# Head and key norms kept as columns of tokens, and the linear recurrence and its neighbours moved to earlier units of mixer 2's projection

## The chip, the cores and the metric

One core of a Trainium2 chip runs the whole program. The metric is the device time of one execution in microseconds (us). TensorE does matmuls, VectorE and ScalarE work elementwise, GpSimd and SyncE here only issue DMAs.

## The reference

512 tokens with 1024 features pass two blocks. The first has two layers: a layer norm with modulation from a vector c, a projection to 22 tiles of 128 features, attention (8 query heads and 2 key heads of 64, each normed over its 64 features and rotated), a short convolution, a Fourier mix, and an output projection with another layer norm. The second has two layers, each feed-forward, mixer, feed-forward. The mixer of its last layer (mixer 2) is the one that the change touches:

```python
q = _axial_rope(_rms_norm(q.reshape(b, s, N_Q_HEADS, HEAD_DIM), q_gain[l]), row_ang, col_ang)
k = _axial_rope(_rms_norm(k.reshape(b, s, N_KV_HEADS, HEAD_DIM), k_gain[l]), row_ang, col_ang)
...
kk = _l2norm(_heads(k * rwkv_k_k, RWKV_HEADS))
y = _rwkv7_scan(rh, decay, kh, vh, kk, a)
xb = _causal_dwconv(lx, lru_conv_w) + lru_conv_b
log_a = -LRU_C * gate_r * jax.nn.softplus(-lru_lambda)
mult = jnp.sqrt(jnp.maximum(-jnp.expm1(2.0 * log_a), 0.0))
hl = _linear_scan(jnp.exp(log_a), mult * gate_i * xb)
y_lru = hl * jax.nn.gelu(ly)
return jnp.concatenate([y_rwkv, y_lru], -1) @ w_out
```

## The kernel before

Features lie on partitions, tokens along the free axis, 512 wide. A weight unit is 128 output features by 1024 inputs. SyncE loads units into a ring of four; ScalarE writes a rounded copy (`high`, L1609), VectorE the remainder (`low`, L2215), and TensorE forms each of the 8 input tiles' product as three matmuls of 512 columns, 24 for a unit (`part` in the projections does some of the 8 tiles, so that other matmuls can stand between its two halves). Every engine's order is written out by hand, and engines meet through counting semaphores (`pe_done`, `act_done`, `dve_done`, `tile_copied`, `unit_used`, `unit_split`).

**Head norms** (`first_block`, both layers). Units 8 to 12 are the key tile and four query tiles of two heads each, number i = 0 to 4. ScalarE evicts unit 8+i and squares it. In the middle of unit 9+i TensorE multiplies the squares by a constant that has 1/64 within a head (`rms`), which leaves the mean on every partition of the head. ScalarE takes the root of 128x512 (`rsd`), VectorE its reciprocal and one multiplication (`normed`, L2414 and L2198), in its turn 8+i, and TensorE at the end of unit 11+i the matmul `rot` of the rotation, which VectorE finishes in `roped`. In layer 0 the turns 0 to 7 of VectorE also hold three products each for the modulation (`ada`, L2391), whose operands come by DMA from GpSimd's queue.

**Mixer 2** (`odd_projection`, 22 units, then `rwkv`). Units 0 to 3 are the input of the linear recurrence (LRU), unit 4 two low ranks, 5 to 8 keys, 9 to 12 values, 13 a gate, 14 to 17 queries, 18 to 21 the gelu input. VectorE evicts each unit (L3004). Around that stand:

- `lru_gates(i)` on TensorE at the end of unit 5+i, two sigmoids of them on ScalarE (banks 6 and 7, so the next gates wait for them); then exponentials (`la`) in unit 10, squares and tanh in 11, relu and roots (`lmult`) in 12, and on VectorE `lru_root` in 11 and `lru_scan` in 13 and 14.
- `low_rank` in units 7 to 9 and their sigmoids; `key_square` in 7 to 9; `key_squares` in the middle of unit 10 sums the squares of a head, four matmuls with 32 output rows; a root of 128x512 (`kksd`) and its reciprocal (`krstd`, L3018); `key_roots` spreads the result at the ends of units 11 and 12, two banks in turn, so the second pair waits for `unit_keys` of the first.
- `cumulate`, `keys_decayed`, `queries_decayed`, `lru_hidden`, `gelu_inner` and `bonus` on VectorE in units 10 to 21 and after them.

`rwkv` first builds the chunk matrices of four token tiles tt (`matrices`), transposes (`tokens`, waits for each `bonus`), and VectorE masks them; `matrices(tt)` waits for the masks of tt-1.

The reader needs these lines most:

```python
def rms(i):
    pe.wait_ge(*act_done("rsq", l, i))
    step(mm(PS[6][:], cst("blk64"), tile(17 + i)), "rms", l, i)
...
def key_squares():
    pe.wait_ge(*act_done("rgate", 2))
    for j in range(4):
        pe.wait_ge(*act_done("kksq", j))
        ins = mm(PS[6][32 * j:32 * j + 32, :], cst("blk1")[:, 32:96:2], tile(22 + j))
```

Of the kernel before, what the change touches and what calls it, by code (L numbers as in the profile page):

```python
# [132 lines left out]
def write_program(nc, known, x_in, w_k, w_d0, w_d1, w_shift, w_ada, c_in, vec_in, cst_in, small_in, dft_in, out):  # L133

    with ExitStack() as ctx:
# [27 lines left out]
        NORM = sb("norm_columns", [P, 12])  # L163
        PS = [ctx.enter_context(nc.psum_tensor(f"bank{i}", [P, T], F32)) for i in range(8)]
# [275 lines left out]
        def _(pe):  # L440
# [79 lines left out]

            def rms_of(norm, *parts):
# [81 lines left out]
            def first_block(l):  # L603
# [33 lines left out]
                for j in range(K0 + 1, FILLING):  # L637
# [6 lines left out]
                    if j - K0 >= 3:  # L644
                        rot(j - K0 - 3)

# [6 lines left out]
                def scores(p):  # L653
                    t, qt = p // 4, p % 4
                    pe.wait_ge(*dve_done("rope", l, t + 1))
                    if p == 0:
                        pe.wait_ge(*act_done("turn", name, 0))
                    if p >= 2:
# [532 lines left out]
            def odd_projection():  # L1191
# [40 lines left out]
                def key_squares():  # L1232
                    pe.wait_ge(*act_done("rgate", 2))
                    for j in range(4):
                        pe.wait_ge(*act_done("kksq", j))
                        ins = mm(PS[6][32 * j:32 * j + 32, :], cst("blk1")[:, 32:96:2], tile(22 + j))
                    step(ins, "kk2")

                def key_roots(j):
# [3 lines left out]
                    step(mm(PS[6 + j % 2][:], cst("pick")[:, col(j)], tile(22)), "kroot", j)  # L1243
# [6 lines left out]
                for j in range(LEAD, N_ODD):  # L1250
                    part(j, 0, 4)
                    if j == LEAD + 1:
                        spread(("pre", name))
                    if j == 7:
                        low_rank(0)
                    elif j == 10:
                        key_squares()
                    part(j, 4, KT)
                    if 5 <= j <= 8:
                        lru_gates(j - 5)  # L1260
# [7 lines left out]
                    elif j in (11, 12):  # L1268
                        key_roots(2 * j - 22)
                        key_roots(2 * j - 21)  # L1270
                    elif j in (20, 21):
                        bonus(2 * j - 40)
                        bonus(2 * j - 39)
# [265 lines left out]
        def _(act):  # L1539
# [126 lines left out]
            def first_block(l):  # L1666
# [14 lines left out]
                for j in range(K0, FILLING):  # L1681
                    evict(j, ACT.Copy)
                    if j < V0:
                        i = j - K0
                        act.wait_ge(*pe_done("rms", l, i))
                        a(tile(17 + i), PS[6][:], ACT.Sqrt, "rsd", l, i, bias=v("eps6"), chain=False)
# [268 lines left out]

            def odd_projection():
# [30 lines left out]
                def gelu_gate(i):  # L1987
                    act.wait_ge(*dve_done("gelu0", i))
                    a(gelu_input(i), gelu_input(i), ACT.Sigmoid, "gelu", i, scale=float(np.sqrt(8 / np.pi)), chain=False)

                for j in range(N_ODD):
                    if j > LEAD:
# [26 lines left out]
                    if 5 <= j <= 8:  # L2019
                        i = j - 5  # L2020
                        act.wait_ge(*pe_done("lgate", i))
# [1446 lines left out]
```

## Time and profile before

| | before |
|---|---|
| median of 3 runs | 2745.77 us (2742.93 to 2746.58) |
| profiled execution, its own time | 2746.36 us |
| its span, first to last instruction | 2744.40 us |
| TensorE busy | 2670.0 us, 97% |
| VectorE busy | 1545.2 us, 56% |
| ScalarE busy | 1028.5 us, 37% |
| mean granted clock of TensorE | 0.991 of full speed |

The profile is one execution; its own time is 0.59 us over the median. In the timeline a row is one or several instructions of one kind; the name left of the arrow is written, those right of it are read; "128\*64 128x512" is 128 contraction rows, 64 output rows, 512 columns. A plain fp32 matmul shows as two records.

### The profile page before, as it was taken

The numbers are of one execution on the slowest core, as the hardware profiler recorded it, in microseconds if no ns is written. First come the engines' busy times: TensorE is split into PE (matmuls) and PEld (weight loads), VectorE is DVE, ScalarE is ACT, GpSimd is POOL, SyncE is SP. The second block draws the span as 40 slices with busy tenths as digits, with TensorE's granted clock in tenths as the row PEclk, the third lists the DMA queues.
The fourth block names the chain that finished last, engine by engine and source line by source line (L and its number), as shares of the span: only waits on it lengthen the run. The fifth ranks groups of instructions, "written<-read, shape, count | busy, mean of one in ns | idle before, by whom it ended". The sixth has DMA issues, their size and how long they took to land.

```text
span 2744.4 us, 38094 instructions
## 1 busy us (share of the span) xinstructions
PE 2670.0 (97%) x15846; PEld 2135.2 (78%) x15846; DVE 1545.2 (56%) x2232; ACT 1028.5 (37%) x1534; POOL 19.0 (1%) x39
## 2 busy tenths in 40 slices
PE   8999999999999999999999999999999898999998
PEld 5766776678888788877888887888876797788886
DVE  6976867575244664645543447424475975653344
ACT  3354536442223354224322334222346422532322
POOL 0100000000000000000000000000000000000000
PEclk9999999999999999999999999999999999999999
DMA  8611321122332321101323232233222100232322
GB/s 339 224 54 67 115 95 61 55 85 87 104 102 75 102 84 40 41 31 62 109 84 114 82 106 90 87 106 100 77 99 70 48 19 2 92 104 87 109 77 69
DMA packets 71451, 243.93 MB, mean 89 GB/s; under 512 B 7921, under 2 KB 8177, under 8 KB 70257
## 3 DMA queue, kind: packets, MB, share of 16 engines
q1 hardware_dynamic: 66240, 222.11, 24.7%
q0 software_dynamic: 5040, 19.40, 1.9%
q8 instruction: 126, 2.06, 0.3%
q14 instruction: 45, 0.36, 0.0%
HBM read 239.38 MB, written 2.10 MB: 88 GB/s over the span
## 4 chain that ended last, share of the span: by engine, by line
PE 88%; DVE 7%; DMA 2%; ACT 2%; issue 1%; SPq 0%; DVEq 0%; ACTq 0%
PE bank L442 86%; DMA work<-w_ada 2%; DVE work L2198 1%; PE bank L674 1%; DVE residual L2198 1%; DVE weights_low L2215 1%; DVE work L2391 1%; ACT work L1543 1%; ACT weights_high L1609 0%; DVE work L2414 0%; ACT normed L1543 0%; DVE work L2530 0%; DMA residual<-x_in 0%; DVE work L2283 0%; DVE constants L3004 0%
## 5 line engine op out<-in xcount | busy, mean ns | idle before, releaser
L442 PE MATMUL bank<-normed,weights_high 128*128 128x512 f32 x4848 | 1530.6, 397 | 11.0 <-ACT normed L1543 11.0
L442 PEld LDWEIGHTS bank<-normed,weights_high 128*128 128x128 f32 x4848 | 904.2, 189 | 234.9 <-issue 51.9
L442 PE MATMUL bank<-normed,weights_low 128*128 128x512 f32 x2424 | 949.3, 392 | 0.0
L1609 ACT ACTIVATE weights_high<-ring 128x1024 fp32r<-128x1024 f32 (+2 forms) x431 | 420.7, 979 | 833.0 <-PE bank L442 830.7
L2215 DVE TENSOR_TENSOR weights_low<-ring,weights_high 128x1024 fp32r<-128x1024 f32 (+2 forms) x431 | 484.0, 1125 | 408.7 <-ACT weights_high L1609 405.2
L442 PEld LDWEIGHTS bank<-normed,weights_low 128*128 128x128 f32 x2424 | 457.6, 189 | 96.2
L442 PE MATMUL bank<-hidden,weights_high 128*128 128x512 f32 x1408 | 433.7, 389 | 0.0
L442 PEld LDWEIGHTS bank<-hidden,weights_high 128*128 128x128 f32 x1408 | 264.5, 188 | 54.7
L2590 DVE TENSOR_TENSOR silu_gate<-bank,rstd 128x512 f32<-128x512 f32 x176 | 120.9, 691 | 325.0 <-PE bank L442 324.9
L442 PE MATMUL bank<-hidden,weights_low 128*128 128x512 f32 x704 | 274.2, 390 | 0.0
L442 PEld LDWEIGHTS bank<-hidden,weights_low 128*128 128x128 f32 x704 | 132.2, 188 | 27.4
L442 PE MATMUL bank<-work 64*64 64x64 f32 (+6 forms) x1600 | 146.2, 316 | 5.5 <-DVE work L3076 4.1
L1543 ACT ACTIVATE work<-bank 128x512 f32<-128x512 f32 (+2 forms) x175 | 97.5, 582 | 112.1 <-PE bank L442 84.7
L442 PEld LDWEIGHTS bank<-work 64*64 64x64 f32 (+2 forms) x1600 | 83.3, 148 | 46.0 <-issue 26.8
L1543 ACT ACTIVATE hidden<-silu_gate 128x512 fp32r<-128x512 f32 x88 | 55.6, 632 | 152.3 <-DVE silu_gate L2596 152.3
L2578 DVE TENSOR_TENSOR hidden<-silu_gate,hidden 128x512 fp32r<-128x512 f32 x88 | 61.0, 693 | 61.5 <-ACT hidden L1543 61.5
L442 PE MATMUL bank<-work,constants 128*128 128x512 f32 (+5 forms) x328 | 73.0, 376 | 17.5 <-DVE work L2198 4.9
L1543 ACT ACTIVATE silu_gate<-bank 128x512 f32<-128x512 f32 (+1 forms) x40 | 23.9, 598 | 111.4 <-PE bank L442 111.4
L1543 ACT ACTIVATE silu_gate<-silu_gate 128x512 f32<-128x512 f32 x88 | 54.5, 619 | 27.9 <-DVE silu_gate L2590 27.9
L442 PEld LDWEIGHTS bank<-work,constants 64*64 64x64 f32 (+2 forms) x328 | 34.3, 156 | 36.2 <-issue 9.3
L1543 ACT ACTIVATE work<-work 128x512 f32<-128x512 f32 (+1 forms) x78 | 47.5, 628 | 39.6 <-DVE work L2525 12.6
L2596 DVE TENSOR_TENSOR silu_gate<-silu_gate 128x512 f32<-128x512 f32 x88 | 60.3, 686 | 0.8
(270 smaller groups left out, 1919.1 us busy)
## 6 DMA issues: line engine op xcount, KB each, us to landing
ring<-w_k SPq DMA_DIRECT2D x303, 512.0 KB, 3.7
ring<-w_d SPq DMA_DIRECT2D x64, 384.0 KB, 3.0
ring<-w_d SPq DMA_DIRECT2D x64, 320.0 KB, 2.9
work<-w_ada POOLq DMA_DIRECT2D x32, 512.0 KB, 6.4
work<-w_shift SPq DMA_DIRECT2D x4, 1024.0 KB, 10.9
work<-w_ada SPq DMA_DIRECT2D x7, 512.0 KB, 17.2
constants<-cst_in SPq DMA_DIRECT2D x1, 2176.0 KB, 21.0
residual<-x_in SPq DMA_DIRECT2D x4, 512.0 KB, 6.5
```

Of the source, the lines that this page charges most:

```text
L442: return pe.matmul(o, lhsT, rhs, start=start, stop=stop, skip_group_check=True)
L674: ins = pe.transpose(PS[4 + s][:, col(st)], probs(p, s)[:, col(st)], cst("ident"))
L1543: ins = nc.scalar.activation(o, i, func, bias=bias, scale=scale, **extra)
L1609: nc.scalar.activation(WH[:, u % SPLIT, 0:w], RING[:, u % SLOTS, 0:w], ACT.Copy).then_inc(unit_high, 1)
L2198: return ve.scalar_tensor_tensor(out=o, in0=a, scalar=s, in1=b, op0=op0, op1=op1)
L2215: ve.tensor_tensor(WL[:, u % SPLIT, 0:w], RING[:, u % SLOTS, 0:w], WH[:, u % SPLIT, 0:w].bitcast(F32), ALU.subtract).then_inc(unit_split, 1)
L2391: d(ve.scalar_tensor_tensor(out=w, in0=w, scalar=v("one"), in1=BIG[:, 22:24, :], op0=ALU.mult, op1=ALU.mult, accum_out=MOD[:, l, 8 * part ...
L2578: d(ve.tensor_tensor(HID[:, 12 + p, :], GATE[:, 2 + p % 2, :], HID[:, p, :].bitcast(F32), ALU.subtract), "hidden", f, q, p, chain=False)
L2590: d(ve.tensor_tensor(GATE[:, 2 * w + p % 2, :], ffn_bank("pair", q, p, w)[:], RSTD[:, 1, :], ALU.mult), "scaled", f, q, p, w, chain=False)
L2596: d(ve.tensor_tensor(GATE[:, 2 + p % 2, :], GATE[:, 2 + p % 2, :], GATE[:, p % 2, :], ALU.mult), "gated", f, q, p, chain=False)
```

## The change

1. **Head norms.** `rms(i)` exchanges its operands: per token tile the squares are the stationary side, so the result has tokens on partitions and the heads in columns (4 matmuls of 128 columns in place of one of 512). Root and reciprocal are of 128x8 in place of 128x512. A new step `rms_spread(i)` at the end of unit 9+i brings the result back to features on partitions: 8 matmuls, each with 64 output rows and 128 columns, into bank 0. It waits for VectorE's reciprocal (`rrms`) and the last `normed`. `normed(i)` comes a turn later and reads bank 0.
2. **Key norms.** `key_squares` becomes 16 matmuls with 128 output rows and 32 columns; root and reciprocal are of 128x32; `key_roots` is 8 matmuls as above in place of one of 512 columns, at the ends of units 11 and 13.
3. **Linear recurrence.** The gates stand at the end of unit 5, the middle and end of 6 and the middle of 7; the exponentials in ScalarE's turn 7, squares and tanh in 8, relu and roots in 9, VectorE's roots in 9, the scans in 10 and 11.
4. **The rest of VectorE's steps** is about a unit sooner; `bonus` on TensorE comes after unit 19 and in the middle of 21. `gelu_inner` and `gelu_gate` of 2 and 3 stand behind the masks of the first token tile.

```diff
+            def spread_heads(bank, columns):
+
+                for tt in range(TT):
+                    for s in range(2):
+                        x = 2 * tt + s
+                        ins = mm(bank[64 * s:64 * s + 64, col(tt)], columns[:, x:x + 1].broadcast_to([P, 64]), cst("ident"))
+                return ins
...
                 def rms(i):
                     pe.wait_ge(*act_done("rsq", l, i))
-                    step(mm(PS[6][:], cst("blk64"), tile(17 + i)), "rms", l, i)
+                    for tt in range(TT):
+                        ins = mm(PS[6][:, col(tt)], tile(17 + i)[:, col(tt)], cst("blk64"))
+                    step(ins, "rms", l, i)
+
+                def rms_spread(i):
+                    pe.wait_ge(*dve_done("rrms", l, i))
+                    if i:
+                        pe.wait_ge(*dve_done("rn", l, i - 1))
+                    step(spread_heads(PS[0], HEAD_NORM[i % 2]), "rspread", l, i)
...
                     if j - K0 >= 3:
                         rot(j - K0 - 3)
+                    if j - K0 - 1 < 5:
+                        rms_spread(j - K0 - 1)
...
-                        ins = mm(PS[6][32 * j:32 * j + 32, :], cst("blk1")[:, 32:96:2], tile(22 + j))
+                        for tt in range(TT):
+                            x = 4 * j + tt
+                            ins = mm(PS[6][:, 32 * x:32 * x + 32], tile(22 + j)[:, col(tt)], cst("blk1")[:, 48:80])
...
-                    step(mm(PS[6 + j % 2][:], cst("pick")[:, col(j)], tile(22)), "kroot", j)
+                    step(spread_heads(PS[6 + j % 2], KEY_NORM[:, 8 * j:8 * j + 8]), "kroot", j)
...
+                    if j in (6, 7):
+                        lru_gates(2 * j - 11)
                     if j == 7:
                         low_rank(0)
                     elif j == 10:
                         key_squares()
+                    elif j == 21:
+                        bonus(2)
+                        bonus(3)
                     part(j, 4, KT)
-                    if 5 <= j <= 8:
-                        lru_gates(j - 5)
+                    if j in (5, 6):
+                        lru_gates(2 * j - 10)
...
                 for j in range(N_ODD):
+                    if j in (6, 7):
+                        lru_sigmoids(2 * j - 11)
                     if j > LEAD:
                         high(u0 + j + SPLIT)
...
-                    if j == 9:
-                        low_rank_gates(3)
-                        key_square(3)
-                        act.wait_ge(*pe_done("kk2"))
-                        a(tile(22), PS[6][:], ACT.Sqrt, "kksd", bias=v("eps6"), chain=False)
-                    elif j == 10:
+                    if j == 7:
                         act.wait_ge(*dve_done("lam"))
                         for i in range(4):
                             act.wait_ge(*act_done("lr", i))
                             a(GATE[:, i, :], tile(i), ACT.Exp, "la", i, scale=LRUV[:, 8 + i:9 + i], chain=False)
-                    elif j == 11:
+                    elif j == 8:
                         for i in range(4):
                             lru_decay_square(i)
                             a(tile(i), tile(i), ACT.Tanh, "ltanh", i, scale=LRUV[:, 12 + i:13 + i], chain=False)
-                        key_decays(0)
-                    elif j == 12:
+                    elif j == 9:
+                        low_rank_gates(3)
+                        key_square(3)
...
+                        act.wait_ge(*pe_done("kk2"))
+                        a(KEY_NORM[:], PS[6][:, 0:T:16], ACT.Sqrt, "kksd", bias=v("eps6"), chain=False)
...
+                    if K0 < j <= V0:
+                        dve.wait_ge(tile_copied, c0 + j)
+                        normed(j - K0 - 1)
                     if K0 <= j < V0:
-                        dve.wait_ge(tile_copied, c0 + j + 1)
-                        normed(j - K0)
+                        reciprocal_rms(j - K0)
```

How the orders move, at two places. First VectorE in layer 0, from the last operation on the modulation (128x8) through turns 8 and 9; `weights_low` is `low`. Before:

```order
L2198 SCALAR_TENSOR_TENSOR modulation<-modulation,vectors 128x8 [waits dve_steps]
L2215 TENSOR_TENSOR weights_low<-ring,weights_high 128x1024 [waits unit_used,unit_high]
L2414 RECIPROCAL work<-work 128x512 [waits act_steps,tile_copied]
L2198 SCALAR_TENSOR_TENSOR work<-work,vectors 128x512 [waits dve_steps]
L2215 TENSOR_TENSOR weights_low<-ring,weights_high 128x1024 [waits unit_used,unit_high,dve_steps]
L2414 RECIPROCAL work<-work 128x512 [waits act_steps,tile_copied,consts_in]
L2198 SCALAR_TENSOR_TENSOR work<-work,vectors 128x512 [waits dve_steps]
```

Now:

```order
L2231 SCALAR_TENSOR_TENSOR modulation<-modulation,vectors 128x8 [waits dve_steps]
L2248 TENSOR_TENSOR weights_low<-ring,weights_high 128x1024 [waits unit_used,unit_high]
L2453 RECIPROCAL head_norm<-head_norm 128x8 [waits act_steps]
L2248 TENSOR_TENSOR weights_low<-ring,weights_high 128x1024 [waits unit_used,unit_high]
L2231 SCALAR_TENSOR_TENSOR work<-work,vectors,bank 128x512 [waits pe_steps,tile_copied,consts_in]
L2453 RECIPROCAL head_norm<-head_norm 128x8 [waits act_steps]
L2248 TENSOR_TENSOR weights_low<-ring,weights_high 128x1024 [waits unit_used,unit_high]
```

The reciprocal keeps its place behind the turn's `low`; the multiplication moved behind the next `low` and now reads TensorE's bank.

Second ScalarE in mixer 2, turns 7 and 8 (`weights_high` is `high`, work<-constants the kept part of a unit, work<-bank the sigmoids of gates or low ranks, work<-work,vectors the squares of keys, silu_gate the exponentials). Before, turn 8:

```order
L1609 ACTIVATE weights_high<-ring 128x1024 [waits unit_used,w_loaded1]
L1543 ACTIVATE work<-constants,modulation 128x512 [waits tile_copied]
L1543 ACTIVATE work<-bank,vectors 128x512 [waits pe_steps]
L1543 ACTIVATE work<-bank,vectors 128x512
L1543 ACTIVATE work<-work,vectors 128x512 [waits dve_steps]
L1543 ACTIVATE work<-bank,vectors 128x512 [waits pe_steps]
L1543 ACTIVATE work<-bank,vectors 128x512
```

Now, from the exponentials at the end of turn 7 to the first squares and tanh of turn 8:

```order
L1571 ACT_TABLE_LOAD [waits act_steps]
L1571 ACTIVATE silu_gate<-work,lru_vectors 128x512 [waits dve_steps]
L1571 ACTIVATE silu_gate<-work,lru_vectors 128x512 [waits act_steps] x3
L1637 ACTIVATE weights_high<-ring 128x1024 [waits unit_used,w_loaded1]
L1571 ACTIVATE work<-constants,modulation 128x512 [waits tile_copied]
L1571 ACTIVATE work<-work,vectors 128x512 [waits dve_steps]
L1571 ACT_TABLE_LOAD
L1571 ACTIVATE work<-bank,vectors 128x512 [waits pe_steps]
L1571 ACTIVATE work<-bank,vectors 128x512
L1571 ACTIVATE work<-silu_gate 128x512 [waits act_steps]
L1571 ACTIVATE work<-work,lru_vectors 128x512
```

The four exponentials, the squares and tanh (three more pairs follow) and two table loads now stand ahead of turn 9.

## Rows read from the trace of the kernel before

**Rows 1.** Timeline, TensorE, layers 0 and 1 (start us, us, engine, line, what, [idle before and releaser]).
```profile
94.04 1.02 PE L442 MATMUL bank<-work,constants 128*128 128x512 f32 x2
...
111.25 1.13 PE L442 MATMUL bank<-work,constants 128*128 128x512 f32 x2 [0.72 <-DVE work L2198]
...
122.68 1.31 PE L442 MATMUL bank<-work,constants 128*128 128x512 f32 x2 [3.95 <-DVE work L2421]
...
380.02 1.02 PE L442 MATMUL bank<-work,constants 128*128 128x512 f32 x2
383.65 1.02 PE L442 MATMUL bank<-work,constants 128*128 128x512 f32 x2
```

**Rows 2.** Timeline, VectorE, layer 0, turns 7 and 8.
```profile
105.83 0.17 DVE L2198 SCALAR_TENSOR_TENSOR modulation<-modulation,vectors 128x8 f32<-128x8 f32 x1
105.92 1.22 DVE L2215 TENSOR_TENSOR weights_low<-ring,weights_high 128x1024 fp32r<-128x1024 f32 x1
107.06 3.35 DVE L2414 RECIPROCAL work<-work 128x512 f32<-128x512 f32 x1
```

**Rows 3.** Timeline, TensorE: existing matmuls of the shapes that come in.
```profile
172.04 3.65 PE L442 MATMUL bank<-work 128*64 128x512 f32 x16
...
1028.49 1.05 PE L442 MATMUL bank<-constants,work 128*128 128x1 f32 x8
1029.40 0.70 PE L442 MATMUL bank<-normed,weights_high 128*128 128x512 f32 x2
...
1088.87 4.54 PE L442 MATMUL bank<-work 128*64 128x128 f32 x64
```

**Rows 4.** Timeline, TensorE, projection of mixer 2, without its units.
```profile
2054.13 1.88 PE L442 MATMUL bank<-work,small_weights 128*128 128x512 f32 x4
...
2085.58 1.99 PE L442 MATMUL bank<-work,small_weights 64*128 64x512 f32 x8
2090.44 1.60 PE L442 MATMUL bank<-work,constants 128*32 128x512 f32 x8
...
2101.39 1.99 PE L442 MATMUL bank<-work,constants 128*128 128x512 f32 x4 [0.95 <-DVE work L3018]
2113.00 3.37 PE L442 MATMUL bank<-work,constants 128*128 128x512 f32 x4 [4.14 <-DVE work L2198]
```

**Rows 5.** Timeline, ScalarE, projection of mixer 2.
```profile
2059.59 1.25 ACT L1543 ACTIVATE work<-bank,vectors 128x512 f32<-128x512 f32 x2
...
2085.75 1.06 ACT L1609 ACTIVATE weights_high<-ring 128x1024 fp32r<-128x1024 f32 x1 [3.75 <-PE bank L442]
...
2087.94 2.40 ACT L1543 ACTIVATE work<-bank,vectors 128x512 f32<-128x512 f32 x4
...
2090.96 1.28 ACT L1543 ACT_TABLE_LOAD   x1
...
2098.08 2.56 ACT L1543 ACTIVATE silu_gate<-work,lru_vectors 128x512 f32<-128x512 f32 x4
...
2103.66 0.61 ACT L1543 ACTIVATE work<-silu_gate 128x512 f32<-128x512 f32 x1
...
2104.79 0.61 ACT L1543 ACTIVATE work<-silu_gate 128x512 f32<-128x512 f32 x1
```

**Rows 6.** Timeline, VectorE, eviction of units 10 and 13.
```profile
2095.03 0.69 DVE L3004 TENSOR_TENSOR constants<-bank,rstd 128x512 f32<-128x512 f32 x1 [5.71 <-PE bank L442]
...
2122.15 0.69 DVE L3004 TENSOR_TENSOR constants<-bank,rstd 128x512 f32<-128x512 f32 x1 [8.64 <-PE bank L442]
```

**Rows 7.** Timeline, TensorE, end of the projection and the first chunks.
```profile
2167.77 1.88 PE L442 MATMUL bank<-silu_gate,constants 128*128 128x512 f32 x4
...
2180.09 3.69 PE L442 MATMUL bank<-work 64*64 64x128 f32 x64 [2.79 <-DVE work L3076]
...
2187.89 1.98 PE L442 MATMUL bank<-work 64*64 64x128 f32 x64 [0.64 <-DVE work L3076]
```

**Rows 8.** Stretches: length; PE, PEld, DVE, ACT, POOL busy; granted clock; DMA share, GB/s.
```profile
2179.00:2181.00 2.00, 0.91 (x18) 0.91 (x21) 2.00 (x6) 0.00 (x0) 0.00 (x0) 0.50 0.00 0
```

More of the change, by code:

```diff
@@ L1267, in odd_projection @@
                         low_rank(3)
[L1268 to L1273, printed above, removed]
+                    elif j in (11, 13):
+                        key_roots(j - 11)
+                        key_roots(j - 10)
+                    elif j == 19:
+                        bonus(0)
+                        bonus(1)
                 pe.wait_ge(tile_copied, c0 + N_ODD)
@@ L1954, in lru_lambda, with gelu_gate @@
                 a(LRUV[:, 0:4], LRUV[:, 0:4], ACT.Exp, "lam", scale=-1.0, chain=False)
+            def gelu_gate(i):
+                act.wait_ge(*dve_done("gelu0", i))
+                a(gelu_input(i), gelu_input(i), ACT.Sigmoid, "gelu", i, scale=float(np.sqrt(8 / np.pi)), chain=False)
             def odd_projection():
@@ L2410, in normed, with reciprocal_rms @@
                 def normed(i):
+                    dve.wait_ge(*pe_done("rspread", l, i))
+                    x = tile(ROPED[i])
+                    d(stt(x, x, v("qg" if i else "kg", l), PS[0][:], ALU.mult, ALU.mult), "rn", l, i, chain=False)
+                def reciprocal_rms(i):
                     dve.wait_ge(*act_done("rsd", l, i))
[L2413 to L2415 removed]
+                    r = HEAD_NORM[i % 2]
+                    d(ve.reciprocal(r[:], r[:]), "rrms", l, i, chain=False)
                 def roped(i):
@@ L3017, in odd_projection @@
                         dve.wait_ge(*act_done("kksd"))
-                        d(ve.reciprocal(tile(22), tile(22)), "krstd", chain=False)
+                        d(ve.reciprocal(KEY_NORM[:], KEY_NORM[:]), "krstd", chain=False)
+                        lru_scan(0)
+                        lru_scan(1)
                         cumulate(0)
                     elif j == 11:
+                        lru_scan(2)
+                        lru_scan(3)
                         cumulate(1)
-                        for i in range(4):
-                            lru_root(i)
                     elif j == 12:
@@ L3045, in odd_projection, with gelu_inner @@
                         queries_decayed(3)
-                    elif j >= 20:
-                        lru_hidden(j - 20)
-                        gelu_inner(j - 20)
-                        bonus(j - 20)
-                for i in (2, 3):
-                    lru_hidden(i)
-                    gelu_inner(i)
-                    bonus(i)
+                    elif j == 20:
+                        for i in (0, 1):
+                            lru_hidden(i)
+                            gelu_inner(i)
+                            bonus(i)
+                    elif j == 21:
+                        for i in (2, 3):
+                            lru_hidden(i)
+                            bonus(i)
+                    if j == 9:
+                        for i in range(4):
+                            lru_root(i)
+            def gelu_inner(j):
+                x = gelu_input(j)
+                dve.wait_ge(*act_done("gelu0", j))
+                dve.wait_ge(*dve_done("lhidden", j))
+                d(stt(x, gelu_square(j), 1.0, x, ALU.add, ALU.mult), "gelu0", j, chain=False)
             def lru_out(j):
@@ L3066, in rwkv @@
                     else:
-                        for j in ((1, 2) if tt == 1 else (3,) if tt == 2 else ()):
-                            lru_out(j)
+                        if tt == 1:
+                            gelu_inner(2)
+                            gelu_inner(3)
+                        lru_out(tt)
                         low(UNIT0["mixout1"] + tt - 1)
```

72 lines of the change are left out of this document (31 added, 41 removed).

## The prediction

> **What bounds the kernel now.** I read the busy times first: TensorE is busy 97% of the span, so whatever it gains or loses goes into the time almost whole, and work on VectorE or ScalarE counts only where TensorE waits for it. Then I read the waits of TensorE at the places of the change. In layer 0 it waits 0.72 us and 3.95 us for VectorE, which does the reciprocals of 3.35 us in a row [rows 1, 2]. In mixer 2 it waits 0.95 us for the reciprocal of the key norms and 4.14 us for the first two unit keys [rows 4]. At the end of the projection VectorE's chain holds it up: from 2167.77, when unit 21 has ended, to 2187.89, when the third chunk's matrices start, 20.1 us pass [rows 7]. A wait costs more than itself. After the one of 2.79 us the granted clock is 0.50, the lower level of 1.2 GHz, and 64 records take 3.69 us that take 1.98 later [rows 7, 8]: 1.7 us more for a long wait.
>
> **A pace for all that follows.** In layer 1 half a unit and a matmul of 512 columns take 3.63 us, 380.02 to 383.65 [rows 1]. Of that the matmul, two records of fp32, is 0.87, since four records with nothing between take 1.88 and their last end reaches some 0.15 further [rows 4]. Half a unit is 2.75 and a unit 5.5.
>
> **Head norms, price on TensorE.** Turning `rms` round leaves 512 columns in all: nothing. `rms_spread` adds 8 matmuls, 16 records of 64 output rows, ten times in all. Two neighbours of that shape run beside each other: 16 records of 512 columns take 3.65 [rows 3], 8 times 0.43 in place of 16. The nearest row in width, 64 records of 128 columns in 4.54, gives 1.1 for 16 [rows 3]; going into the other shape and back I put at 0.2, an estimate by the 0.2 that the 3.65 has over 8 times 0.43. I take 1.3 each. The bounds are 0.9 (a quarter of 3.65) and 2.0 (no overlap, 16 times 0.11 from the records of one column, plus 0.2).
>
> **Layer 0.** This step decides. `rms_spread(0)` waits for the reciprocal of VectorE's turn 8, and TensorE asks for it at the end of unit 9. `rms(0)` starts at 94.04 in the middle of that unit [rows 1], so the unit ends at 94.04 + 3.63 = 97.7. VectorE is then far behind: its turns 0 to 7 hold the modulation, whose last operation starts at 105.83, and after the turn's `low` (1.22) the reciprocal starts at 107.06 [rows 2]. Nothing in that chain is shortened by the change. A reciprocal of 8 columns ends about 0.2 later (an operation of 8 columns takes 0.17 [rows 2]), so TensorE waits from 97.7 to 107.3, 9.6 us, all units behind it too. Before, the first result of VectorE that it needed was `normed(0)` at the end of unit 11, two units later. The sum for layer 0: 9.6 for the wait, 1.7 for the clock, 5 × 1.3 = 6.5 for the spreads, less 0.72 + 3.95 + 1.7 for the waits that go. They go since the reciprocals of 3.35 are gone and every later `rot` finds `normed` done: **+11.4 us**. With the wait over, ScalarE's root, VectorE's `low` and the small reciprocal fit into the half unit between `rms` and `rms_spread` (0.6 even for 512 columns [rows 5], 1.22 and 0.2, against 2.75), so the four later spreads don't wait.
>
> **Layer 1.** VectorE is in step there. Five spreads, no wait: **+6.5 us**.
>
> **Mixer 2, to the end of unit 21.** Gates 1 move to the middle of unit 6 and need the banks that ScalarE empties by its two sigmoids of gates 0. Gates 0 start at 2054.13; the middle of unit 6 is 2 × 0.87 + 2.75 later, 2058.6. The sigmoids run from 2059.59 to 2060.84, where they stand in ScalarE's turn 5 before as now [rows 4, 5]: +2.3. From there all of TensorE is 2.3 later; unit 9, which ended at 2085.58 after all four gates [rows 4], ends at 2087.9, unit 7 two units and a `low_rank` (half of 1.99) before, 2075.7 or so.
>
> `key_squares`, in the middle of unit 10, waits for ScalarE's last square of a key. Before it found it nearly done. Now ScalarE has more ahead of it. From 2075.7 it does three turns of high, kept and square (2085.75 to 2087.94 is 2.19 each, 6.6), a fourth square (0.6), eight sigmoids (four start to start in 2.3 us, 4.6), four exponentials (2.56), four pairs of square and tanh (2103.66 to 2104.79, 4 × 1.13 = 4.5) and two table loads (2 × 1.28 = 2.6) [rows 5]. That is 21.5 us: 2097.2, the sigmoids that it waits for first at 2095.4. TensorE is there at 2087.9 + 1.99 + 2.75 = 2092.7: a wait of 2.7 before the first matmuls. They are 32 records of 128 output rows; records of that shape with a single column start 0.11 apart (eight from 1028.49 to 1029.40 [rows 3]), so 32 take 3.5, in place of the 1.7 from 2090.44 to half a unit (2.75) before the eviction at 2095.03 [rows 4, 6]. Together 2.7 + 3.5 − 1.7 = +4.5, and 1.7 for the clock. The Trainium skill (TensorE: Matmul & The Clock Gate, Back-to-back issue gap) gives some 60 cycles to a matmul of up to 64 columns; by that the 32 would take 0.8 us and the total be 2.7 lower. The row with 0.11 decides for me, as every record here brings new weights of 128 columns.
>
> Four `key_roots` at 1.3 for 0.87: +1.7. What goes: 0.95 and 4.14, and the low clock after it (2113.00 to the eviction at 2122.15 is 9.15, for 2 × 0.87 + 5.5: 1.9) [rows 4, 6], and a small wait of `bonus`: −7.2. The second pair of roots behind unit 13 finds the keys within 1 us, since the scans now lie ahead of them on VectorE: 0, up to +1. Sum: 2.3 + 4.5 + 1.7 + 1.7 − 7.2 = **+3.0 us**.
>
> **The end of the projection.** Two of the `bonus` matmuls move before the end of unit 21, so I compare from unit 21 with all four done: before, 2167.77 + 1.74 = 2169.5 to 2187.89, 18.4 us [rows 7]. Now VectorE has, behind that point, one eviction, two pairs of `lru_hidden` and `bonus`, one `lru_out` and eight masks. With 0.69 for an operation of 512 columns [rows 6], 0.6 or so from start to start, and half for a mask of 256, that is 0.7 + 4 × 0.6 + 0.7 + 8 × 0.35 = 6.6; the matrices of tile 1 start then. VectorE goes on with two gelu steps, a `lru_out`, a `low` and eight masks, 1.3 + 0.6 + 1.2 + 2.8 = 5.9, waits some 0.3 for a transpose, and the matrices of tile 2 start. That is 12.9, all of it worked out from those rows, in place of 18.4: **−5.5 us**. The later cycles don't change; VectorE had slack there for one more `lru_out`.
>
> **Two waits between.** The wait of 2.3 at gates 1 and one of about 2.2 before the matrices of tile 1 are shorter than any after which I saw the low clock (2.79). I count half of 1.7 for each: **+1.7 us**.
>
> **Sum.** 11.4 + 6.5 + 3.0 − 5.5 + 1.7 = +17.1 us on the profiled execution's 2746.36: 2763.5. It lay 0.6 above the median of the runs, so I say **2763 us**.
>
> **The rivals.**
>
> *Spreads without overlap, slower still.* Fourteen spreads at 2.0 in place of 1.3: +9.8, **2773 us**. For it: each switch of shape may wait for the array to empty. The skill says so (TensorEngine Tiling (Array Packing), Key Properties: changing the tiling mode drains TensorE); the 3.65 in rows 3 holds such a switch and bounds it at some tenths. Against it: these rows. 0.14.
>
> *ScalarE keeps up in mixer 2.* If its chain to the last square is shorter than TensorE's (it decides at 2092.7), the waits of 2.7 and 2.3 and the low clocks there go, −2.7 − 1.7 − 2.3 − 0.85: **2755 us**. For it: ScalarE is busy only 37% of the span. Against it: the sum of 21.5 us has no idle in it. 0.12.
>
> *Not slower: no answer is asked for before it is there.* The mechanism is that VectorE's turn 8 in layer 0 comes in time; it decides whether its reciprocal is over by 97.7. Then 9.6 + 1.7 go, and in mixer 2 the waits of the rival above: 2763 − 11.3 − 7.5 = **2744 us**, 1.4 under the median; with the spreads at 0.9 it would be 2739. For it: the work removed from VectorE, ten reciprocals of 3.35, is far more than what is added. Against it: all of that work lies behind 105.83 in layer 0, and the modulation ahead of it waits for DMAs that nothing here speeds up. 0.09, split evenly over faster and the same.
>
> **How the numbers follow.** The forecast has 0.65. 2751 to 2773 holds it with the bounds of a spread (ten of them and four at 0.9 are −5.6) and most of the second and third case. 0.2% is 5.5 us, about what a measurement of this kernel can tell from no change; slower by more than that starts at 2751.3, and all cases but the last are there. Faster 0.05, the same 0.06, slower 0.89.
>
> **What would show it.** In the profile after: a wait of TensorE of about 9.6 us for a VectorE reciprocal at 97.7 in layer 0, and none in layer 1; ten groups of 16 records of 64 output rows, each about 1.3 us; in mixer 2 a wait near 2.3 us at the second gates, one of 2 to 3 us ahead of the 32 records of the key squares, no wait of 0.95 or 4.14; the matrices of tile 1 at 6.6 us after the end of unit 21. The forecast is wrong if layer 0 shows no long wait, if a spread takes 2 us, or if ScalarE's last square of keys comes before TensorE is in the middle of unit 10.

## The result, and the profile after

| | before | after |
|---|---|---|
| median of 5 runs | 2744.42 us (2742.0 to 2746.58) | 2757.46 us (2754.98 to 2761.96) |
| profiled execution, its own time | 2746.36 us | 2754.98 us |
| TensorE busy | 2670.0 us | 2679.2 us |
| VectorE busy | 1545.2 us | 1509.3 us |

The ratio of the runs is 1.0049, 95% interval 1.0038 to 1.0060: **slower by 13 us**, where 17 on a base of 2746.4 was forecast. The busy times of the page after:

```profile
PE 2679.2 (97%) x16146; PEld 2148.8 (78%) x16146; DVE 1509.3 (55%) x2232; ACT 1024.6 (37%) x1534; POOL 19.0 (1%) x39
```

VectorE has 36 us less to do, and the whole is slower even so; TensorE has 9 us more. Layers 0 and 1 on TensorE, first the ends of the two stretches in the kernel before (the first scores of layer 0, rms(0) and the first scores of layer 1):

```profile
145.72 1.13 PE L442 MATMUL bank<-work 64*128 64x512 f32 x4
...
363.70 1.02 PE L442 MATMUL bank<-work,constants 128*128 128x512 f32 x2
...
408.64 1.13 PE L442 MATMUL bank<-work 64*128 64x512 f32 x4
```

The same timeline of the kernel after:

```profile
93.39 1.05 PE L444 MATMUL bank<-constants,work 128*128 128x128 f32 x8
...
105.32 1.97 PE L444 MATMUL bank<-constants,head_norm 128*64 128x128 f32 x16 [8.14 <-DVE head_norm L2453]
...
110.76 1.05 PE L444 MATMUL bank<-constants,work 128*128 128x128 f32 x8
...
114.48 1.09 PE L444 MATMUL bank<-constants,head_norm 128*64 128x128 f32 x16
118.36 1.05 PE L444 MATMUL bank<-constants,work 128*128 128x128 f32 x8
...
154.23 1.13 PE L444 MATMUL bank<-work 64*128 64x512 f32 x4
...
372.27 1.05 PE L444 MATMUL bank<-constants,work 128*128 128x128 f32 x8
...
375.99 1.09 PE L444 MATMUL bank<-constants,head_norm 128*64 128x128 f32 x16
...
423.30 1.13 PE L444 MATMUL bank<-work 64*128 64x512 f32 x4
```

From rms(0) to the first scores, layer 0 took 145.72 − 94.04 = 51.7 us [rows 1] and takes 60.8, **+9.2**. The wait is 8.14, not 9.6. After it the stretch from spread to the next rms takes 5.44 (105.32 to 110.76) in place of the later 3.88 (114.48 to 118.36): 1.6 of low clock. Layer 1 went from 44.94 to 51.03, **+6.1**, without a wait. VectorE in layer 0, against [rows 2]:

```profile
103.93 1.22 DVE L2248 TENSOR_TENSOR weights_low<-ring,weights_high 128x1024 fp32r<-128x1024 f32 x1
105.07 0.19 DVE L2453 RECIPROCAL head_norm<-head_norm 128x8 f32<-128x8 f32 x1
```

The reciprocal is the small one of 0.19 now, but it stands at the same place, 1.1 us behind a `low` that starts at 103.93. What makes VectorE late is mostly its own work: it is busy for 29.9 of the 33 us from 60 to 93, with products of 1.28 us each, and its waits for the products' operands by DMA are 4.8 us in all up to here. Without them the reciprocal would stand at about 100.4 (an estimate: 105.2 less 4.8), still 3 us behind the moment at which TensorE asks for it, 105.32 − 8.14 = 97.18. Mixer 2 on TensorE, against [rows 4]:

```profile
2063.36 1.88 PE L444 MATMUL bank<-work,small_weights 128*128 128x512 f32 x4
...
2070.21 2.62 PE L444 MATMUL bank<-work,small_weights 128*128 128x512 f32 x4 [2.20 <-ACT work L1571]
...
2076.39 1.88 PE L444 MATMUL bank<-work,small_weights 128*128 128x512 f32 x4
...
2098.88 1.99 PE L444 MATMUL bank<-work,small_weights 64*128 64x512 f32 x8
...
2106.82 5.17 PE L444 MATMUL bank<-constants,work 128*128 128x32 f32 x32 [3.02 <-ACT work L1571]
...
2122.03 1.97 PE L444 MATMUL bank<-constants,key_norm 128*64 128x128 f32 x32
...
2135.11 1.97 PE L444 MATMUL bank<-constants,key_norm 128*64 128x128 f32 x32
```

Here are the wait of 2.20 at the second gates (6.18 us to the third, where two matmuls and half a unit are 4.5: 1.7 of low clock), the wait of 3.02 and the 32 records of the key squares, and two pairs of key roots without a wait. And the tail, against [rows 7]:

```profile
2179.73 1.88 PE L444 MATMUL bank<-silu_gate,constants 128*128 128x512 f32 x4
...
2185.16 1.98 PE L444 MATMUL bank<-work 64*64 64x128 f32 x64 [0.78 <-DVE work L3038]
...
2191.25 1.98 PE L444 MATMUL bank<-work 64*64 64x128 f32 x64 [2.21 <-DVE work L3118]
...
2196.84 1.98 PE L444 MATMUL bank<-work 64*64 64x128 f32 x64 [0.79 <-DVE work L3118]
```

Unit 21 ends at 2185.16 − 0.78 = 2184.38 with all bonuses done. The matrices of tile 1 come 6.9 us later, those of tile 2 12.5 later, in place of 18.4. From the first gates to there mixer 2 takes 133.5 us (2063.36 to 2196.84) in place of 133.8 (2054.13 to 2187.89): nothing.

These pieces give 9.2 + 6.1 − 0.3 = 15.0, yet the two executions are 8.6 apart. Most of the difference, 5.4 us, lies where nothing was changed: from the first scores of layer 1 to the first gates of mixer 2 the kernel before took 1645.5 us and the one after 1640.1 (last section). Another 0.65 lies ahead of rms(0), which starts at 93.39 for 94.04.

### The profile page after: what moved, and what is told of

The parts are those of the page before. It is cut to its first block, busy times and chain, and to the rows that moved or that the text cites. A ratio compares the mean times of both kernels' runs of the same rounds, so it can differ in the third digit from the quotient of the medians.

```text
span 2753.2 us, 38698 instructions
## 1 busy us (share of the span) xinstructions
PE 2679.2 (97%) x16146; PEld 2148.8 (78%) x16146; DVE 1509.3 (55%) x2232; ACT 1024.6 (37%) x1534; POOL 19.0 (1%) x39
## 4 chain that ended last, share of the span: by engine, by line
PE 89%; DVE 6%; ACT 2%; DMA 2%; issue 1%; SPq 0%; DVEq 0%; ACTq 0%
PE bank L444 88%; DMA work<-w_ada 1%; PE bank L695 1%; DVE work L2231 1%; DVE residual L2231 1%; ACT work L1571 1%; DVE weights_low L2248 1%; DVE work L2424 1%; ACT weights_high L1637 0%; ACT normed L1571 0%; DVE work L2570 0%; ACT silu_gate L1571 0%; DMA residual<-x_in 0%; DVE work L3118 0%; DVE work L2316 0%
## 5 line engine op out<-in xcount | busy, mean ns | idle before, releaser
L444 PEld LDWEIGHTS bank<-hidden,weights_low 128*128 128x128 f32 x704 | 132.1, 188 | 27.4
L444 PE MATMUL bank<-work,constants 64*64 64x64 f32 (+4 forms) x292 | 55.0, 341 | 7.5 <-ACT work L1571 3.1
L444 PEld LDWEIGHTS bank<-constants,work 128*128 128x128 f32 (+1 forms) x560 | 52.2, 173 | 12.5 <-ACT work L1571 4.4
```

Source lines behind the costliest of these rows:

```text
L444: return pe.matmul(o, lhsT, rhs, start=start, stop=stop, skip_group_check=True)
```

## The experiments

Ratios are to the kernel before on the same chip, with 95% intervals; 0.001 is 2.7 us. "Layer 0" is from rms(0) to the first scores, "mixer 2" from the first gates to the matrices of tile 2, in the profiled execution. E1, E3 and E4 start from the kernel after, E2 and F4 from the kernel before.

| | ratio | layer 0 | mixer 2 |
|---|---|---|---|
| before | | 51.7 | 133.8 |
| after | 1.0049 (1.0038 to 1.0060) | 60.8 | 133.5 |
| E1 mixer 2's part alone | 1.0004 (0.9995 to 1.0013) | 52.0 | 134.9 |
| E2 head norms alone | 1.0057 (1.0044 to 1.0070) | 63.9 | 134.6 |
| E3 early answers | 1.0014 (1.0006 to 1.0023) | 51.0 | 134.8 |
| E4 recurrence a turn later | 1.0034 (1.0021 to 1.0047) | 63.6 | 128.3 |
| F1 E1 with E4's places | 0.9979 (0.9970 to 0.9988) | 51.6 | 128.5 |
| F2 F1 with old key norms | 0.9991 (0.9983 to 1.0000) | 52.0 | 132.1 |
| F3 E1 with old key norms | 1.0013 (1.0004 to 1.0022) | 52.0 | 134.8 |
| F4 gelu move alone | 0.9992 (0.9984 to 1.0001) | 51.9 | 131.6 |
| G1 F1, squares between products | 0.9975 (0.9966 to 0.9984) | 51.5 | 127.8 |
| G2 G1, scans behind the keys | 0.9978 (0.9969 to 0.9987) | 51.8 | 128.1 |
| G3 G2, layer 0 with new norms | 0.9974 (0.9964 to 0.9984) | 51.0 | 128.1 |
| G4 whole change, repaired | 0.9993 (0.9984 to 1.0002) | 51.0 | 128.1 |

**E1 and E2: which half loses.** E1 puts the old head norms back into the changed kernel, E2 puts the new ones alone into the kernel before:

```diff
-                    for tt in range(TT):
-                        ins = mm(PS[6][:, col(tt)], tile(17 + i)[:, col(tt)], cst("blk64"))
-                    step(ins, "rms", l, i)
+                    step(mm(PS[6][:], cst("blk64"), tile(17 + i)), "rms", l, i)
...
-                    if j - K0 - 1 < 5:
-                        rms_spread(j - K0 - 1)
```

> The changed kernel with the head norms of both layers put back as they were, so parts 2 to 4 of the change alone. Theory (sum of the two profiles): the head norms are the whole loss, 9.2 us in layer 0 (from rms(0) to the first scores 60.84 in place of 51.68) and 6.1 us in layer 1 (51.03 in place of 44.94); mixer 2 gives about as much as it takes (133.48 in place of 133.76 from the first gates to the matrices of tile 2). Then 2744 us, within 0.1% of the kernel before, and the mixer 2 of the changed kernel again: waits of 2.2 at the second gates and 3.0 at the key squares. Rival: mixer 2 by itself loses some us that the low clock in the even mixer of the kernel before hides in the pair of profiles; then 2748 us or more. In both, the tail from the end of unit 21 to the matrices of tile 2 takes 12.6 us.

> The kernel before with the new head norms of both layers and nothing else, so part 1 alone. Theory: +9.2 in layer 0 and +6.1 in layer 1, 15.3 us, about 2759.7. Rival: the stretch of low clock in the even mixer (1030 to 1042 in the profile of before, worth 5.1 us, not there in that of after) goes because the head norms shift what follows; then +10, about 2754.6, and its profile has a granted clock of 1.0 there.

E1 is 1.1 us over the kernel before and within the error of it; E2 is 15.6 over it (12.1 to 19.2). The head norms are the whole loss. E2's time is that of its theory; in its trace the stretch of low clock from 1030 to 1042 is gone as its rival has it (granted clock 1.00), but its runs as a whole don't show the 5 us less that this would give. E2's wait for VectorE in layer 0 was 10.07 us and E4's 9.67: it moves by 2 us from trace to trace, and VectorE's waits for DMAs in its turns up to there move with it (4.8 us in the kernel after, 6.8 in E2, 5.8 in E4). The low clock behind this wait moves too: from the first spread to the next rms pass 5.44 us in the kernel after, 6.55 in E2 and 6.68 in E4, for 3.88 at the full clock.

**E3: is it the place of VectorE's answers?**

```diff
                             ada(2 + m // KT, m % KT)
+                            if m == 18:
+                                reciprocal_rms(0)
+                            elif m == 22:
+                                dve.wait_ge(tile_copied, c0 + K0 + 1)
+                                normed(0)
+                                reciprocal_rms(1)
```

> The changed kernel with VectorE's first two reciprocals of layer 0, and the first multiplication, put between the modulation's products of turns 6 and 7, so that TensorE finds them at the ends of units 9 and 10. Theory: the wait of 8.1 us and the low clock after it (1.6) go, nothing takes their place: 2757.5 less 9.7 is 2747.8 us. Rival: VectorE stays late, since the products wait for their operands by DMA, and the second spread waits instead, 3 us and the low clock with it: 2752.5 us. If a wait of a third of the length in the same place cost nothing, 2749 to 2750.

The first and the second spread and the first scores, with no wait between:

```profile
97.78 1.09 PE L444 MATMUL bank<-constants,head_norm 128*64 128x128 f32 x16
...
105.38 1.09 PE L444 MATMUL bank<-constants,head_norm 128*64 128x128 f32 x16
...
145.10 1.13 PE L444 MATMUL bank<-work 64*128 64x512 f32 x4
```

The ratio is 0.0035 below the changed kernel's, 9.6 us for a forecast of 9.7. Three operations were moved and none removed, so the loss of layer 0 lay in their place and not in the work of the new norms. Layer 0 at 51.0 is even 0.7 below the kernel before: there the five spreads cost less than the waits of 0.72 and 3.95 and the low clock that the old norms had.

**E4 and F1: the recurrence too early for ScalarE.** Gates and sigmoids at the ends of units 5 to 8 again, the other steps one turn later than the change has them:

```diff
-                    if j in (5, 6):
-                        lru_gates(2 * j - 10)
+                    if 5 <= j <= 8:
+                        lru_gates(j - 5)
...
-                    if j == 7:
+                    if j == 8:
                         act.wait_ge(*dve_done("lam"))
```

> The changed kernel with the gates of the linear recurrence where they were (ends of units 5 to 8), its exponentials in ScalarE's turn 8, squares and tanh in 9, relu and roots in 10, VectorE's roots in 10 and scans in 11 and 12; all else is kept. Theory: the waits of 2.2 us at the second gates and 3.0 us at the key squares go with the low clock behind each (1.7 each): 2757.5 less 8.6 is 2748.9 us, and the 32 records of the key squares, 5.17 us before, take 3.5 at the full clock. Rival 1: those 5.17 are their price at any clock, and 1.7 less is won: 2750.6. Rival 2: the scans now stand ahead of the keys of the second pair, and that pair of roots waits 2 us or more: 2751 to 2753.

> The kernel with mixer 2's part of the change alone (old head norms), and the recurrence's steps a turn later with the gates at the ends of units 5 to 8, as in the run before it on the changed kernel. Theory: in the traces that placement took 128.3 us from the first gates to the matrices of tile 2, where the change took 133.5 to 134.9; so 5 to 6 us less than mixer 2 alone (2745.9), 2740 to 2741 us, and faster than the kernel before. Rival: the placement is worth only the wait of 2.2 and 3.0 us less the new wait of 2 us at the second pair of roots, 3.2: 2742.7.

In E4 and F1 both waits of mixer 2 go, and it takes 128.3 and 128.5 us. F1, the change without its head norms, is **5.8 us faster than the kernel before** (3.3 to 8.2), and 6.9 below E1 by the ratios, 6.4 by the traces, where 5 to 6 were expected. E4 stands 4.1 below the changed kernel, not 8.6, for two reasons. One is its rival 2, a new wait of 1.97 at the second pair of roots. The other neither theory held: the low clock stays though TensorE waited only 0.17. F1's timeline (key squares, two pairs of roots) and its stretches (columns as in [rows 8]):

```profile
2085.51 4.59 PE L444 MATMUL bank<-constants,work 128*128 128x32 f32 x32 [0.17 <-ACT work L1558]
...
2100.69 1.97 PE L444 MATMUL bank<-constants,key_norm 128*64 128x128 f32 x32
...
2115.72 1.97 PE L444 MATMUL bank<-constants,key_norm 128*64 128x128 f32 x32 [1.96 <-DVE work L2214]
```

```profile
2086.00:2088.00 2.00, 2.00 (x21) 2.00 (x20) 0.00 (x0) 2.00 (x5) 0.00 (x0) 1.00 0.01 4
2088.00:2090.00 2.00, 2.00 (x13) 2.00 (x12) 0.00 (x0) 2.00 (x5) 0.00 (x0) 0.56 0.00 0
2090.00:2092.00 2.00, 2.00 (x6) 1.61 (x6) 0.00 (x0) 1.98 (x4) 0.00 (x0) 0.50 0.00 0
```

TensorE is busy without a gap from 2086 on and its weight load until 2090, with 32 small records in a row, and the granted clock falls to 0.50. At the full clock the 32 took 3.76 us (E4, whose clock fell at about their end).

**F2 and F3: is it the records or the wait?** The key norms in their old form, once without and once with the wait ahead of them (the edit also puts their root, reciprocal and `key_roots` back):

```diff
-                        for tt in range(TT):
-                            x = 4 * j + tt
-                            ins = mm(PS[6][:, 32 * x:32 * x + 32], tile(22 + j)[:, col(tt)], cst("blk1")[:, 48:80])
+                        ins = mm(PS[6][32 * j:32 * j + 32, :], cst("blk1")[:, 32:96:2], tile(22 + j))
```

> The same, and the key norms in their old form too (four matmuls of 512 columns with 32 output rows, root and reciprocal of 128x512, roots by one matmul each), so the moves of parts 3 and 4 alone. Theory: the key squares cost 1.7 us in place of 3.8 and the 1.5 of low clock that follow the small records; the four roots 0.87 in place of 1.04 each. 4.3 us less: 2736 us. Rival: the reciprocal of 3.35 us stands in VectorE's turn 10 ahead of the recurrence's roots and scans, VectorE comes later to the unit keys, and TensorE waits up to 3 us more at the roots: 2739 us, about no gain.

> Mixer 2's part of the change with its own places for the gates and the recurrence, old head norms, and the key norms in their old form. TensorE still waits 3.0 us for ScalarE ahead of the key squares. What tells the theories apart is the stretch from the start of the key squares to the end of unit 11, which holds 1.7 of squares and 8.25 of units at the full clock: theory A (the low clock there comes with the 32 small records, which have it also behind a wait of 0.17 us) 9.95 us; theory B (it comes from the wait) 11.5. It was 15.2 to 16.8 with the new form. In us: A 2745.9 less 5.9 is 2740.0, B 2741.5, either up to 3 more if TensorE now waits for the reciprocal of 3.35.

F3, key squares and first roots:

```profile
2090.52 1.08 PE L444 MATMUL bank<-work,constants 128*32 128x512 f32 x6 [3.03 <-ACT work L1558]
...
2105.43 1.98 PE L444 MATMUL bank<-work,constants 128*128 128x512 f32 x4 [0.94 <-DVE work L3030]
```

From the first square to the end of unit 11, less a wait of 0.68 within, are 2105.43 − 0.94 − 2090.52 − 0.68 = 13.3 us; it was 10.0 in the kernel before. So the low clock comes with a long wait and without any small record, which is theory B, though 3.3 us of it and not 1.5. In F2, old form and no long wait (0.17, and 0.70 within), the granted clock stays at 1.00 and the stretch is 10.5. But F2 as a whole is 3.3 us slower than F1. That is its rival, and worse, for the rival had about no gain: VectorE's big reciprocal is back ahead of the keys, and TensorE waits twice, 3.22 and 4.11, where F1 waits once, 1.96, with low clock behind the second wait (3.75 us for 1.98):

```profile
2100.02 1.98 PE L444 MATMUL bank<-work,constants 128*128 128x512 f32 x4 [3.22 <-DVE work L3026]
...
2117.05 3.75 PE L444 MATMUL bank<-work,constants 128*128 128x512 f32 x4 [4.11 <-DVE work L2212]
```

**G1: the same records, not in a row.**

```diff
+                    if j == 10:
+                        for q in range(4):
+                            key_squares(q)
+                            part(j, 4 + q, 5 + q)
```

> The best version so far (mixer 2 alone, recurrence a turn later; 0.9979 of the kernel before), with the four groups of key squares put one by one ahead of the last four products of unit 10 in place of all together. Same instructions. Theory: the low clock behind the squares comes with 32 small records in a row, even where nothing waited; between matmuls of 512 columns it does not come, and from the first square to the end of unit 11 pass 8.25 + 3.5 to 3.8 = about 12 us in place of 13.6 and 15.2: 1.5 to 3 us less, ratio 0.997. Rival: the clock falls there for another reason (the work before it), and the stretch stays at 13.6 or more; ratio 0.998.

```profile
2090.19 1.08 PE L444 MATMUL bank<-constants,work 128*128 128x32 f32 x8 [0.17 <-ACT work L1562]
...
2091.89 0.97 PE L444 MATMUL bank<-constants,work 128*128 128x32 f32 x8
...
2102.21 1.97 PE L444 MATMUL bank<-constants,key_norm 128*64 128x128 f32 x32
...
2118.24 1.97 PE L444 MATMUL bank<-constants,key_norm 128*64 128x128 f32 x32 [2.96 <-DVE work L2218]
```

2102.21 − 2090.19 = 12.02 us with the granted clock at 1.00 throughout; G2 to G4 have 12.0 too. It was 15.2 in F1. Of the 3.2 us, 1.0 goes into a longer wait of the roots (2.96 for 1.96), and in this trace some into a low clock at the matrices of tile 1 (3.58 us for 64 records). By the runs G1 is 1 us better than F1, which the intervals can't tell from none.

**G2, G3, G4.** G2 moves the scans behind the unit keys; G3 is G2 with new norms and E3's places in layer 0 alone; G4 has them in both layers.

```diff
                     elif j == 11:
                         cumulate(1)
-                        lru_scan(0)
-                        lru_scan(1)
```

> The same, and the recurrence's scans behind the unit keys in VectorE's turns (0 and 1 in turn 12, 2 and 3 in turn 13). Theory: VectorE reaches the unit keys of 0 and 1 3.7 us sooner, and the wait of 1.96 us ahead of the second pair of roots goes: 2 us less than the run before it, ratio 0.9965 or less. Rival: VectorE, which has no idle time from turn 12 to 20, is that much later at the end of the projection, and the wait comes back at the bonus steps: no gain.

> The same, and in layer 0 alone the new head norms with VectorE's first answers between the modulation's products; layer 1 keeps the old ones. Theory: layer 0 takes 51.0 us from rms(0) to the first scores in place of 51.7 to 52.0, so 0.7 to 1 us less than the run before it. Rival: the same within the error, since the five spreads (6.1 us in layer 1) eat what the waits for VectorE cost with the old norms (4.7 us and a low clock).

> All four parts of the change kept, with all repairs: the first answers of layer 0 between the modulation's products, the recurrence a turn later, key squares between products, scans behind the unit keys. Theory: this is the run before it plus the five spreads of layer 1, 6.1 us; below the kernel before only if the repairs of mixer 2 hold: ratio 0.9985. Rival: new head norms in both layers cost what they cost in the changed kernel without the wait, and the total is no better than the kernel before: 1.000.

G2, the second pair of roots and the second of the first bonuses:

```profile
2115.52 1.97 PE L444 MATMUL bank<-constants,key_norm 128*64 128x128 f32 x32 [0.49 <-DVE work L2218]
...
2153.58 2.08 PE L444 MATMUL bank<-silu_gate,constants 128*128 128x512 f32 x2 [2.12 <-DVE silu_gate L2218]
```

The rival of G2 holds: the wait falls from 2.96 to 0.49 and comes back as 2.12 at the bonus. G3 is 0.7 us faster in layer 0 by the trace, and within the error by the runs. G4 has all four parts of the change and is 15 us below the changed kernel (0.9993 to 1.0049), level with the kernel before; it lies between its theory (0.9985) and its rival (1.000) and settles neither. The 5.2 us from G3 to G4 are layer 1's spreads (6.1 by the trace).

**F4: the tail.** In the kernel before, `gelu_inner` and `gelu_gate` of 2 and 3 go behind the masks of the first tile:

```diff
                     else:
-                        for j in ((1, 2) if tt == 1 else (3,) if tt == 2 else ()):
-                            lru_out(j)
+                        if tt == 1:
+                            gelu_inner(2)
+                            gelu_inner(3)
+                        lru_out(tt)
```

> The kernel before with one move alone: the gelu steps of VectorE and ScalarE for 2 and 3 behind the masks of the first token tile. Theory: VectorE reaches those masks 1.2 us sooner (two operations of 0.6), so the matrices of tile 1 start 1.2 us sooner, and if the shorter wait of 1.6 us is not followed by the low clock, another 1.7: 1.2 to 2.9 us, 2741 to 2743. The rest of the 5.8 us of the tail in the changed kernel then comes from VectorE being sooner (bonus in unit 21, recurrence earlier). Rival: the gelu move is the whole of it, 5.8 us: 2738.

```profile
2168.13 1.88 PE L442 MATMUL bank<-silu_gate,constants 128*128 128x512 f32 x4
...
2186.11 1.98 PE L442 MATMUL bank<-work 64*64 64x128 f32 x64 [0.64 <-DVE work L3078]
```

2168.13 + 1.74 to 2186.11 is 16.2 us in place of 18.4. The runs give 2.2 too, but their interval (0.9984 to 1.0001) doesn't rule out none. So by the trace the move is a good third of the tail's 5.9. The wait of 2.79 did not shrink to 1.6, since what stands ahead of it waits for VectorE too and came sooner. That VectorE's earlier steps bring the other two thirds fits, but was not tried apart, so it is not shown.

## Why the prediction was right, point by point

- **Layer 0, +11.4.** Measured +9.2 in the profile after, +12.2 and +12.0 in E2 and E4. The mechanism (the place of the answer behind the modulation, not the work) is shown by E3. The wait was forecast at 9.6 and is 8.1, 10.1 and 9.7: one trace of before could not give it closer than about 2 us. The low clock behind it was forecast at 1.7 and is 1.6, 2.7 and 2.8. The reason for VectorE's lateness was given too narrowly as the DMAs: its waits for them are 5 to 7 us, and its own products would make it late without them.
- **Layer 1, +6.5.** +6.1 in every trace with the new norms. A spread is 3.88 less half a unit, 1.1 to 1.2, where I took 1.3 within 0.9 and 2.0. The Trainium skill (TensorEngine Tiling (Array Packing), Key Properties) has each change of tiling mode drain TensorE. Whatever that costs is inside these 1.2.
- **Mixer 2 to the end of unit 21, +3.0, and a half of 1.7 for the gates.** Measured 121.0 (2063.36 to 2184.38) less 115.5 (2054.13 to 2169.65, from the 0.99 before the matrices at 2170.64 in the timeline of before), **+5.5**. The waits were right (2.20 for 2.3, though the rows give 2.2 there: 2060.84 − 2058.6; and 3.02 for 2.7). Mis-sized were the low clocks: 1.7 behind the gates where I counted half of it, and some 3 behind the key squares where I took 1.7 (6.96 us for squares and low clock together, forecast 5.2; 8.6 in E1). Mis-sized the other way were the key roots: 13.08 us pass from the first pair to the second, less two units of 5.5 is 1.04 for a root and not 1.3, so +0.7 for four and not +1.7. The term of 3.5 for the 32 records held: 3.76. The Trainium skill (TensorE: Matmul & The Clock Gate, Back-to-back issue gap) has some 60 cycles for a matmul this narrow, and says that its formula leaves the weight load out. The 0.8 us that the prediction worked out from it don't fit the 3.76.
- **Tail, −5.5.** Measured −5.9 (−5.8 from 2169.65, where the point above ends), the matrices of tile 1 at 6.9 for 6.6.
- **Sum.** By the pair of traces 15.0 for 17.1: layer 0 came out 2.2 lower and mixer 2 with the gates' low clock 1.7 higher, so that some of the closeness is luck. Of the 8.5 us between 2763.5 and the profiled execution's 2754.98, 5.4 are the base: the execution of before held them in an untouched stretch, and that of after has not. Against the medians the miss is 5.5: 1.4 by the base, which two more runs brought from 2745.77 to 2744.42, and 4.1 by the difference, 13.0 for 17.1. Of these the terms above explain 2.1. The other 2 are open; in E2, with 12.2 in layer 0, the runs gave 15.6.
- **Rivals.** "Spreads without overlap" is out, since a spread took 1.2 us and not 2.0. "ScalarE keeps up" is out by the waits, and true as a repair: E4's later places let it. "Not slower" failed where I said, at VectorE's turn 8; with the answer in time (E3) it came to +3.8 us, since layer 1's spreads stay.

## What to carry to other kernels

Making a step on the path cheap for one engine gains nothing if its place in that engine's order stays behind other long work; here VectorE had 36 us less work, TensorE asked for its answer two units sooner and waited 8 to 10 us for it, and moving three instructions took that back. A step moved to an earlier place needs every engine's queue at that place added up, ScalarE's as much as VectorE's. And one profiled execution is a base only as good as its own low clocks: compare the stretches that a change doesn't touch first.

## What the hardware showed that I had not expected

**A low clock without a wait.** In the mixer of the layer before, which the change doesn't touch, TensorE is busy all through and yet falls to the lower level, in stretches of the kernel before (columns as in [rows 8]):

```profile
1030.00:1034.00 4.00, 4.00 (x22) 3.72 (x21) 0.05 (x1) 0.00 (x0) 0.00 (x0) 0.67 0.00 0
1034.00:1038.00 4.00, 4.00 (x14) 3.49 (x14) 0.00 (x0) 0.00 (x0) 0.00 (x0) 0.50 0.00 0
1038.00:1042.00 4.00, 4.00 (x11) 3.09 (x10) 3.20 (x6) 2.35 (x3) 0.00 (x0) 0.55 0.16 20
```

Small matmuls of one column run ahead of this stretch ([rows 3], 1028.49), but F1 runs the same ones there (1028.06) and has no low clock behind them. It is in five of the fourteen profiled executions (before, F4, G1, G2, G3), where the first scores of layer 1 to the first gates of mixer 2 take 1645.1 to 1645.5 us. In eight of the others it is 1640.1 to 1640.7; in E4 it is 1643.4, with a lower mean clock (0.87 for 0.96 in E3) between 1230 and 1270. All five have the old norms in layer 1 and none of the five with the new ones has it; four with the old ones haven't it either. Each kernel has one trace, so whether it belongs to a kernel or to an execution is not shown. The runs speak for the execution: the 11 of F4 go from 2738.3 us at a mean clock of 0.995 to 2747.1 at 0.991, and its profiled one, with the stretch, has 2743.6 at 0.991; the profiled ones of E1 and F3, without it, lie 4.0 and 4.5 us under the medians of their kernels.

**The same wait, two prices.** A wait of 2.2 us at the second gates was followed by 1.7 us of low clock in the kernel after and in E3, and by less than 0.1 in E1 (4.56 us to the third gates) and F3. The one at the matrices of tile 1, 2.2 too, has 64 records behind it that take 1.98 us in all in the kernel after and 3.46 in E1. The clock behind a wait of this length can't be told from its length alone.

**Small matmuls in a row.** The low clock followed 32 records of 32 columns with a wait of 0.17 ahead (E4, F1), and it followed four matmuls of 512 columns with a wait of 3.0 ahead (F3). It followed neither four of 512 without a long wait (F2) nor the same 32 records between products (G1 to G4). What else it depends on was not tried.
